# A two-block transformer in split fp32 on one core: start by half blocks, closing norm shared with GpSimd, up products left in PSUM, ten early low halves on VectorE

## The reference

```python
def swiglu(x, w_gu, w_down):
    gate, up = jnp.split(x @ w_gu, 2, axis=-1)
    return (jax.nn.silu(gate) * up) @ w_down
...
    x = x + 0.5 * rms_norm(swiglu(rms_norm(x, ffn1_pre_g[l]), ffn1_w_gu[l], ffn1_w_down[l]), ffn1_post_g[l])
    y = hybrid_mixer(rms_norm(x, mix_pre_g[l]), ...)
    x = x + rms_norm(y, mix_post_g[l])
    x = x + 0.5 * rms_norm(swiglu(rms_norm(x, ffn2_pre_g[l]), ffn2_w_gu[l], ffn2_w_down[l]), ffn2_post_g[l])
...
    h_lat = layer_norm(DEEPNORM_ALPHA * h_lat + m_lat[5] * f_lat, ln_g[i, 1], ln_b[i, 1])   # the last one closes the program
```

## Time and profile before

| what | before |
|---|---|
| median of three runs | 2794.41 us (2793.37 to 2795.77) |
| the profiled execution | 2799.06 us |
| its span, first to last instruction | 2797.2 us |
| mean granted TensorE clock | 0.998 |
| PE busy | 2766.6 us, 99% |
| DVE, ACT, POOL busy | 1893.6, 1237.3, 402.0 us |

### The profile page before, as it was taken

One profiled execution on the slowest core, in us unless ns is written; L12 is line 12 of the kernel. 1 busy time (PEld: TensorE's weight loads), 2 busy tenths in 40 slices (PEclk: granted clock), 3 DMA queues, 4 the chain that ended last, 5 costly groups with the idle time before them and its releaser, 6 DMA issues.

```text
span 2797.2 us, 42563 instructions
## 1 busy us (share of the span) xinstructions
PE 2766.6 (99%) x16554; PEld 2459.0 (88%) x16554; DVE 1893.6 (68%) x3430; ACT 1237.3 (44%) x2248; POOL 402.0 (14%) x219
## 2 busy tenths in 40 slices
PE   9999999999999999999999999999999999999998
PEld 8888896988888888888888999999997787989898
DVE  7788788858895653444435896666686636778686
ACT  5332358642233552332314653344355546545353
POOL 2243300023332011011011000000001323000000
PEclk9999999999999999999999999999999999999999
DMA  6565512236554211111011112222223121222322
GB/s 204 184 189 188 166 64 83 84 104 221 188 191 134 77 54 61 38 61 61 31 61 50 43 54 82 61 68 72 72 76 102 50 76 54 75 83 91 106 91 83
DMA packets 86024, 267.91 MB, mean 96 GB/s; under 512 B 9152, under 2 KB 18752, under 8 KB 85568
## 3 DMA queue, kind: packets, MB, share of 16 engines
q1 hardware_dynamic: 85824, 265.20, 29.6%
HBM read 261.49 MB, written 2.10 MB: 94 GB/s over the span
## 4 chain that ended last, share of the span: by engine, by line
PE 87%; DVE 7%; DMA 3%; ACT 2%; issue 2%; SPq 0%; DVEq 0%; ACTq 0%
PE ps L2072 27%; PE ps L2073 27%; PE ps L2074 27%; DMA t_raw<-in_gu 2%; DVE t_wlo L2764 2%; PE ps L2351 1%; PE ps L2335 1%; PE ps L2324 1%; ACT t_whi L2394 1%; DMA t_x<-in_x 0%; PE ps L2216 0%; DMA t_raw<-in_dn 0%; PE ps L2208 0%; DVE t_raw L2773 0%; PE ps L2267 0%
## 5 line engine op out<-in xcount | busy, mean ns | idle before, releaser
L2072 PE MATMUL ps<-t_h,t_whi 128*128 128x512 f32 (+2 forms) x2152 | 727.3, 338 | 5.0 <-DVE t_wlo L2755 1.9
L2073 PE MATMUL ps<-t_h,t_wlo 128*128 128x512 f32 (+2 forms) x2152 | 721.3, 335 | 0.0
L2074 PE MATMUL ps<-t_h,t_whi 128*128 128x512 f32 (+2 forms) x2152 | 721.1, 335 | 0.0
L2394 ACT CAST t_whi<-t_raw 128x1024 fp32r<-128x1024 f32 (+3 forms) x449 | 368.4, 830 | 565.7 <-PE ps L2074 369.4
L2072 PEld LDWEIGHTS ps<-t_h,t_whi 128*128 128x128 f32 x2152 | 408.3, 190 | 50.3 <-issue 9.9
L2073 PEld LDWEIGHTS ps<-t_h,t_wlo 128*128 128x128 f32 x2152 | 408.5, 190 | 36.5 <-issue 1.2
L2074 PEld LDWEIGHTS ps<-t_h,t_whi 128*128 128x128 f32 x2152 | 408.3, 190 | 35.4
L2072 PE MATMUL ps<-t_hid,t_whi 128*128 128x256 f32 (+2 forms) x1320 | 428.4, 325 | 1.9 <-DVE t_hid L3058 1.7
L2073 PE MATMUL ps<-t_hid,t_wlo 128*128 128x256 f32 (+2 forms) x1320 | 426.1, 323 | 0.0
L2074 PE MATMUL ps<-t_hid,t_whi 128*128 128x256 f32 (+2 forms) x1320 | 425.5, 322 | 0.0
L2764 DVE TENSOR_TENSOR t_wlo<-t_raw,t_whi 128x512 fp32r<-128x512 f32 (+3 forms) x360 | 321.4, 902 | 106.9 <-ACT t_whi L2394 104.0
(11 more groups left out here) (355 smaller groups left out, 4840.6 us busy)
## 6 DMA issues: line engine op xcount, KB each, us to landing
t_raw<-in_gu SPq DMA_DIRECT2D x174, 512.0 KB, 3.4
t_raw<-in_ada SPq DMA_DIRECT2D x96, 512.0 KB, 3.6
t_raw<-in_dn SPq DMA_DIRECT2D x52, 512.0 KB, 4.2
t_raw<-in_dn SPq DMA_DIRECT2D x24, 384.0 KB, 3.4
t_raw<-in_ret_v SPq DMA_DIRECT2D x16, 512.0 KB, 3.5
t_raw<-in_ret_qk SPq DMA_DIRECT2D x16, 512.0 KB, 3.3
t_raw<-in_ret_g SPq DMA_DIRECT2D x16, 512.0 KB, 3.4
t_raw<-in_ret_o SPq DMA_DIRECT2D x16, 512.0 KB, 3.8
```

The costliest lines, as they stand in the source:

```text
L2072: e.matmul(out, whi, xlo, start=first, stop=False, skip_group_check=shared)
L2073: e.matmul(out, wlo, xhi, start=False, stop=False, skip_group_check=shared)
L2074: return e.matmul(out, whi, xhi, start=False, stop=last, skip_group_check=shared)
L2394: e.copy(m.block(0, it.slot, n), m.raw(it)).then_inc(*S["hi"].of(j))
```

## The change

1. **Start by halves.** SP now brings, after the parameters, x chunks 0 to 3, block 0's first half, block 1's first half, then x chunks 4 to 7 and the two second halves. PE multiplies k0 to 3 of block 0, k0 to 3 of block 1, then k4 to 7 of each (`begun`). ACT's and DVE's items for the two blocks are separate for each half. x of tokens 256 to 511 comes in two transfers instead of one.
2. **Early low halves.** EARLY = 10: the low halves of blocks 0 to 9 are all made by DVE, so POOL's first is later, and the turns after it fall on other blocks.
3. **Up products stay in PSUM.** For the 41 up products of 512 tokens (in f1, f2 and two in f4) DVE writes the product with the gate back into the same PSUM bank, ACT rounds from PSUM, and DVE's low half reads PSUM in place of the SBUF temporary. The bank is free after that low half, where it was free after the multiplication.
4. **Closing norm.** ACT copies the mean row from PSUM into SBUF (lead_copy), and POOL subtracts it from chunks 5, 6 and 7; DVE does chunk 0 after the copy, 1 to 4 behind the diagonal.
5. **The planner's model of a DMA.** A transfer is taken to last 1270 ns for each 1024 columns after a latency of 2000 ns (it was 3300 in all); the orders on DVE, ACT and POOL move with it.

```diff
@@ -38,7 +38,8 @@
 GATE = 4608
 COND, ADA_OUT = 6656, 8704
 HALVED = (0, 1)
-SPARED = ()
+EARLY = 10
+SPARED = (5, 6, 7)
 HEAD_ORDER = (0, 4, 1, 5, 2, 6, 3, 7)
 
 
@@ -239,7 +240,7 @@
             takes = 150 + 2.2 * n
             lasts = takes + 60
         else:
-            takes, lasts = 480, 3300
+            takes, lasts, table = 480, 1270 * n / 1024, 2000
         it, piece = self.here
         self.ops[self.engine].append(Op(self.engine, it, piece, self.waits, takes, lasts, table))
         self.waits = []
@@ -358,10 +359,10 @@
                         break
                     doing[engine].popleft().done = True
                     takes, lasts = op.takes, op.lasts
-                    if op.table is not None and op.table != table:
+                    if engine == "scalar" and op.table is not None and op.table != table:
                         table, takes, lasts = op.table, takes + 1283, lasts + 1283
                     if engine == "sync":
-                        landed = max(t + lasts, landed + 1270)
+                        landed = max(t + op.table, landed) + lasts
                         lasts = landed - t
                     free[engine] = t + takes
                     insort(events, free[engine])
@@ -522,7 +523,15 @@
 
         j = take_coming()
         where[j] = slot
-        if chains or state["begin"] or state["held"] is not None or j < len(known) and known[j][0][0] in ("dn3", "dn4"):
+        if j in HALVED:
+            low[j] = "lo_dve"
+            if j == HALVED[-1]:
+                for half in range(2):
+                    for i in HALVED:
+                        put("prep", j=i, slot=where[i], after=after, lo="lo_dve", q="", half=half)
+                        put("prep_lo", j=i, half=half)
+            return
+        if j < EARLY or chains or state["begin"] or state["held"] is not None or j < len(known) and known[j][0][0] in ("dn3", "dn4"):
             low[j] = "lo_dve"
         else:
             turn["low"] = turn.get("low", 0) + 1
@@ -595,12 +604,17 @@
         held = [block(sp[0], sp[1]) for sp in specs]
         for si, (t0, n) in enumerate(segs):
             force_tokens(t0, n)
-            groups = []
+            groups, begun = [], {}
+            if si == 0:
+                for (_, _, nk, src, outs), j in zip(specs, HALVED):
+                    begun[j] = bank()
+                    put("mm", w=j, slot=where[j], lo=low[j], base=0, nk=nk, ks=(0, 1, 2, 3), src=src, t0=t0, n=n, bank=begun[j], po=0,
+                        before=[])
             for (_, _, nk, src, outs), j in zip(specs, held):
                 ready(j)
-                b = bank()
+                b = begun[j] if j in begun else bank()
                 groups.append(put("mm", w=j, slot=where[j], lo=low[j], base=0, nk=nk, src=src, t0=t0, n=n, bank=b, po=0,
-                                  before=seat(b, outs[0][1], len(items))))
+                                  before=seat(b, outs[0][1], len(items)), ks=range(4 if j in begun else 0, nk)))
                 tick(nk * (n + 32) / 800)
             for g, j, (_, _, _, _, ((_, _, post),)) in zip(groups, held, specs):
                 if si == len(segs) - 1:
@@ -821,7 +835,8 @@
         free(keys, ("ps", ("rs", "l11v", 1)))
         put("root_diag", inst="l11v", s=1, off=off, after=after, col=col)
         put("root_row", inst="l11v", s=1, off=off, bank=b)
-        for c in range(DC):
+        put("lead_copy", bank=row)
+        for c in (*SPARED[::-1], *range(SPARED[0])):
             put("lead_z", c=c, bank=row, pool=c in SPARED)
         for c in range(DC):
             put("ln_apply", inst="l11", ln=3, c=c, s=1, bank=b)
@@ -908,12 +923,15 @@
 
             def up_post(k, pi=pi, over_hid=over_hid):
                 def post(g):
-                    off, after, keys = tmp("b", g.n)
+                    turned = f == "f3" and pi == len(parts) - 1 and g.n == 512
+                    stays = g.kind == "mm" and g.n == 512 and not turned
+                    off, after, keys = (0, [], []) if stays else tmp("b", g.n)
+                    if stays:
+                        owner[g.bank] = [("hid_lo", (f, pi, k, g.t0 // 256))]
                     put("up", f=f, key=(f, pi, k, g.t0), g=g.id, bank=g.bank, po=g.po, t0=g.t0, n=g.n, k=k, pitch=pitch,
                         slot=gate_slot[f, pi, k, g.t0], off=off, after=after, over=over_hid, scaled=bool(scaled),
-                        turned=f == "f3" and pi == len(parts) - 1 and g.n == 512,
-                        los=[(f, pi, k, s) for s in range(g.t0 // 256, (g.t0 + g.n) // 256)])
-                    put("up_lo", f=f, t0=g.t0, n=g.n, k=k, pitch=pitch, off=off,
+                        turned=turned, stays=stays, los=[(f, pi, k, s) for s in range(g.t0 // 256, (g.t0 + g.n) // 256)])
+                    put("up_lo", f=f, t0=g.t0, n=g.n, k=k, pitch=pitch, off=off, bank=g.bank, po=g.po, stays=stays,
                         los=[(f, pi, k, s) for s in range(g.t0 // 256, (g.t0 + g.n) // 256)])
                     free(keys, ("hid_lo", (f, pi, k, g.t0 // 256)))
                 return post
@@ -2448,6 +2467,11 @@
         w.wait_ge("ps", "lead_shift")
         e.activation(m.sm(it.col, 2), m.root_columns(it.bank), ACT.Square).then_inc(
             *S["lead_shift"].of(0))
+
+    def lead_copy(it):
+        w.wait_ge("ps", "lead_mean")
+        w.wait_ge("ps", "lead_row")
+        e.copy(m.acc(1, 3), m.PS[:, it.bank, 0:256]).then_inc(*S["lead_copy"].of(0))
 
     def lead_sqrt(it):
         r = m.ST[:, it.col:it.col + 2]
@@ -2511,7 +2535,7 @@
     def up(it):
         w.wait_ge("drain_dve", it.g)
         wait_all(it.over)
-        e.copy(m.hid(0, it.k, it.pitch, it.t0, it.n), m.tmp(it.off, it.n)).then_inc(*S["hid_hi"].of(it.los[0]))
+        e.copy(m.hid(0, it.k, it.pitch, it.t0, it.n), m.ps(it) if it.stays else m.tmp(it.off, it.n)).then_inc(*S["hid_hi"].of(it.los[0]))
 
     def down_f(it):
         if it.pi == 0:
@@ -2931,6 +2952,9 @@
         x = m.x(it.c, 256, 256, "l11")
         w.wait_ge("ps", "lead_row")
         w.wait_ge("x_mid", ("l11", it.c, 1))
+        if it.c:
+            w.wait_ge("root_dve", ("diag", "l11v", 1))
+        w.wait_ge("lead_copy", 0)
         e.tensor_tensor(x, x, m.PS[:, it.bank, 0:256], ALU.subtract).then_inc(*S["x_mid"].of(("l11z", it.c)))
 
     def root_diag(it):
@@ -3039,7 +3063,7 @@
             e.tensor_tensor(s, m.ps(it), m.rs(it.t0, it.n), ALU.mult).then_inc(*S["drain_dve"].of(it.g))
 
     def up(it):
-        s, t = m.at(GATE + it.slot * 512, it.n), m.tmp(it.off, it.n)
+        s, t = m.at(GATE + it.slot * 512, it.n), m.ps(it) if it.stays else m.tmp(it.off, it.n)
         w.wait_ge("ps", it.g)
         if it.scaled:
             w.wait_ge("gate_pool", (it.f, *it.los[0][1:3], it.t0))
@@ -3053,7 +3077,7 @@
             *S["drain_dve"].of(it.g, ("up", it.f, *it.los[0][1:3], it.t0)))
 
     def up_lo(it):
-        t = m.tmp(it.off, it.n)
+        t = m.ps(it) if it.stays else m.tmp(it.off, it.n)
         w.wait_ge("hid_hi", it.los[0])
         e.tensor_tensor(m.hid(1, it.k, it.pitch, it.t0, it.n), t, m.hid(0, it.k, it.pitch, it.t0, it.n), ALU.subtract).then_inc(
             *S["hid_lo"].of(*it.los))
@@ -3456,6 +3480,14 @@
         a = m.tmp(it.offs[2], it.n)
         e.tensor_tensor(a, a, m.tmp(it.offs[3], it.n), ALU.add).then_inc(*S["ret_pool"].of(("sb", it.h, it.t0)))
 
+    def lead_z(it):
+        if it.pool:
+            x = m.x(it.c, 256, 256, "l11")
+            w.wait_ge("lead_copy", 0)
+            w.wait_ge("root_dve", ("diag", "l11v", 1))
+            w.wait_ge("x_mid", ("l11", it.c, 1))
+            e.tensor_tensor(x, x, m.acc(1, 3), ALU.subtract).then_inc(*S["x_pool"].of(("l11z", it.c)))
+
     def na_setup(it):
         wait_all(it.after)
         e.memset(m.at(NZERO, 256), 0.0).then_inc(*S["bm"].of("zero"))
```

More of the change, by code:

```diff
@@ L2018, in serve @@
             x_all, x_in = m.X[:, :].rearrange("p (c t) -> p c t", c=DC), dram["x"].rearrange("c p t -> p c t")
-            e.dma_start(x_all[:, :, 256:512], x_in[:, :, 256:512]).then_inc(*S["d_x1"].of(0))
+            for half in range(2):
+                some = slice(half * 4, half * 4 + 4)
+                e.dma_start(x_all[:, some, 256:512], x_in[:, some, 256:512]).then_inc(*S[f"d_x1{half}"].of(0))
         elif it.kind in ("prep", "ada", "load"):
```

52 lines of the change are left out of this document (24 added, 28 removed).

## The result

The changed kernel takes 2802.12 us (median of 13 runs, 2800.72 to 2806.68), the kernel before 2794.41 (13 runs, 2792.88 to 2798.46): a ratio of 1.0028, interval 1.0020 to 1.0036, so 7.7 us slower where 6.7 faster was forecast. The profiled execution of the change took 2801.49 us, its span 2799.7.

The account below looks back on a forecast made before the run. The prediction took TensorE as the bound, busy 2766.6 of 2797.2 us. Terms 1.0 + 2.35 + 0.3 + 2.6 + 0.45 = 6.7 us took the profiled 2799.06 to 2792.4, hence a median of 2787.7 us, range 2784.0 to 2794.0.

Parts of the forecast that it names:

- Planner's model and moved rows: Rows moved on DVE, ACT and POOL everywhere, PE's in the mixer: 0, between -1.9 and +1.9 us.
- the bill of the ten early low halves: First 40 us: two more low halves on DVE make three other places late, together -1.25 us.
- Clock, 2 x 1.7 us: Slow PE clock behind the gaps at 33.03 and 872.62 us, 1.7 us each, expected to go with them.
- Start and early low halves: First 40 us: sooner first product and half-block order +1.0 us; POOL's early low half gone from beside a sum +2.35.
- second gap: Start, boundary between the first and second halves: some PE wait stays, 0.2 us taken, 0 to 0.9.
- the first sum's row: First 40 us, DVE's new order: the row of the first sum is late next, 0.2 us.
- the second sum's wait: First 40 us: the second row sum of f1 is late behind one more low half on DVE, 0.4 us.
- the wait of 0.65 for block 3's bank: First 40 us: bank of block 3's second half late, its up multiplication waiting for POOL and a silu table.
- 620 us, +0.3: Near 620.80 us: a shorter low half reading PSUM lets a matmul follow at usual spacing, +0.3 us.
- End of f2, +2.6: Last hidden slice of f2: PE's wait falls from 1.7 to 0.8 us and the 1.7 slow-clock loss goes.
- Closing norm, +0.45: End of the kernel: sooner reciprocal 0.15 us and fewer lead_z on DVE 0.3; bounds +0.6 and -1.9.
- The rival on the slower side: Start: ten low halves make DVE the bound, POOL's lead_z hold DVE at the end; 2800.2 us, chance 0.09.

Follow-up runs that it names:

- turns_alone: The kernel before with the DVE/POOL turns of all low halves swapped and no early low halves: 2801.88 us, ratio 1.0028.
- old_model: The changed kernel with the planner's old model of a DMA: 2798.53 us, ratio 1.0017 against the kernel before.
- turns_and_model: The changed kernel with later blocks' turns as before and the planner's old DMA model: 2789.62 us, ratio 0.9990 against the kernel before.
- same: The kernel before, unedited, run again for a second trace: 2794.86 us, ratio 1.0002 against the kernel before.
- change_turns_kept: The changed kernel with the turns of the later blocks swapped back to those of before: 2794.01 us, ratio 0.9995 against the kernel before.
- model_alone: The kernel before with the planner's new model of a DMA and nothing else: 2795.40 us, ratio 1.0010.

## Why the prediction was wrong

- **Planner's model and moved rows, "0, between -1.9 and +1.9", "at nothing, since DVE has a third of its time free": this step failed**, and with it the bill of the ten early low halves, which ends at 40 us and puts nothing on the turns that fall on other blocks after them. DVE was free on average, and its rows moved by a place or two; but at single places a sum that waited for its DMA, or an instruction that POOL's low half held, now stood ahead of what PE waits for, and at 744 us that is a gap of 2.71 us. By the traces the change falls back 1.5 us at 83, 0.8 at 204, 1.1 at 525, 3.0 at 741, 0.8 at 1550, four times 0.3 in the retention mixer, 0.4 at 2070 and at 2359 and 2.9 in f4, some 12 us; it wins 1.7 at the start, 1.2 from 420 to 515, 0.4 at 620, 0.7 at the end of f2 and 0.4 in the closing norm. turns_alone shows that the swap of turns by itself costs 7 us. old_model shows that the new model costs the change 3.6. Its trace falls back at the places of the turns too, but by 1.0 at 741 and 0.2 in f4; it lies 3.3 over its median, with 2.9 lost at the end of f2. What the rest of the change is worth, turns_and_model shows: 3.4 us of the 6.7. I had compared orders only by how far rows moved, not by what waits in them and what POOL does beside them.
- **Clock, 2 x 1.7 us: sized from one execution that is not the usual one.** The rows were right for their execution; in the second one the gaps at 33 and 870 us are 1.6 and 0.6 and the clock stays at 1.00. The excess of 4.65 us over the median that the prediction itself names was made of the two largest terms of its sum, and should have been taken off them. (The prediction calls the two waits the largest; PE waits longer, 3.0 us, for the parameters at the start, in both kernels.)
- **Start and early low halves, +1.0 and +2.35, of which 1.7 was clock.** Without it 1.65; measured 1.7 us (PE's first matmul on a hidden slice at 80.26 in `same`, 78.52 in the change). Its first matmul of 512 columns comes 2.1 us sooner, but PE's row of the norm then follows behind it. First product 0.6 sooner than in the first trace (0.4 said), second gap 0.59 (0.2 said), the first sum's row 0.79 (0.2 said), the second sum's wait 0.23 (0.4 said), and the wait of 0.65 for block 3's bank did not come. The total held; its parts did not all. L2908 took 0.97 us rather than 0.4: POOL's gate products stand beside it.
- **620 us, +0.3:** 0.4, though turns_alone has 0.4 there as well. **End of f2, +2.6, of which 1.7 was clock:** without it 0.9; 0.7 in the trace of the change, which is less than the 1.1 by which the two traces of the kernel before differ there. L3082 at 682 ns was as said. What the prediction takes from the Trainium skill, SBUF — State Buffer, section Who interferes with whom, on two SBUF inputs agrees once more with the trace: the low half of weights at the end of f2, two SBUF operands, lasts 2.28 us beside POOL in the change. The prediction did not ask it of the conditioning sums, which also have two SBUF operands and last 2.33 us at 83 us. That one SBUF input does not contend, as the prediction has it, the section says only of instructions outside VectorE's two-port modes; here the diagonal in model_alone, with one SBUF operand of 128x128, took 2.18 us beside POOL. In which mode it ran no run shows.
- **Closing norm, +0.45:** from the start of PE's last high-by-high product of the down blocks to the end of the span 12.36 us in `same`, 11.96 in the change and in change_turns_kept: 0.4. POOL did not hold DVE.
- **The rival on the slower side** (DVE bound at the start) was the wrong mechanism: the start gained. The loss lay in f1, f2 and f4 and between them, far behind the block 10 to which the edit reaches, and had no rival.

## What to carry to other kernels

A constant that only touches the first blocks can flip an alternation for all that follow; compare the order of each engine not by how far rows moved but by which instruction now stands ahead of one that the critical engine waits for, whether it has a wait of its own, and what the engine that can hold it does beside it. Take the terms of a sum from an execution whose time is the median's: here the excess of the profiled one was made of its gaps and slow stretches, and they could not be saved from the usual run. An alternation like this one is a free parameter, so try both phases before judging the rest of a change.
